# A two-layer mixture-of-experts block: how the gather's rows are copied out, where the seat tables are made, and the order around the router

## What is computed

```python
scores = softmax(x @ w_router + b_router)            # 16 experts in 4 groups of 4
g_sel = argmax(group_score)                          # group_score: sum of a group's two largest
top_w, top_i = top_k(scores within g_sel, 2)         # gate weights, renormalised
for e in range(16):
    h = silu(x @ w_gate[e]) * (x @ w_up[e])          # 1024 -> 512
    y = y + gate[:, e:e+1] * (h @ w_down[e])         # 512 -> 1024
```

## Time and profile before

| | us |
|---|---|
| median of 3 runs | 2279.32 |
| lowest, highest | 2276.93, 2283.09 |
| the profiled execution | 2278.92 |
| its span in the trace | 2277.1 |

### The profile page before, as it was taken

The page is one execution under the profiler, slowest core; times in us unless marked ns, Lnnn a source line. Parts: engine busy times, 40 slices in busy tenths (PEclk is TensorE's granted clock), DMA queues, the critical chain, the costliest instruction groups (busy, mean ns, idle before and its releaser), DMA issues.

```text
span 2277.1 us, 31229 instructions
## 1 busy us (share of the span) xinstructions
PE 2220.8 (98%) x13248; PEld 1916.0 (84%) x13248; DVE 1612.7 (71%) x1577; ACT 1286.8 (57%) x1360; POOL 57.9 (3%) x71
## 2 busy tenths in 40 slices
PE   8999999999999999999999999999999999799997
PEld 7888989788888889897888998887777998687775
DVE  6765855777477557466774666589999666689997
ACT  5434644554344446445543544578887555488885
POOL 1000100000000001000000000000000000100000
PEclk9999999999999999999999999999999999899999
DMA  7755443455555554434664555479998554399995
GB/s 243 218 186 169 148 139 126 163 186 187 193 174 185 188 180 134 152 129 164 199 191 168 181 185 185 141 283 384 385 382 330 181 185 167 131 338 383 388 374 198
DMA packets 309952, 490.93 MB, mean 216 GB/s; under 512 B 15504, under 2 KB 205120, under 8 KB 309808
## 3 DMA queue, kind: packets, MB, share of 16 engines
q1 hardware_dynamic: 305712, 475.35, 61.2%
q0 software_dynamic: 3104, 10.38, 1.6%
q10 hardware_dynamic: 992, 3.15, 0.4%
HBM read 487.40 MB, written 1.44 MB: 215 GB/s over the span
## 4 chain that ended last, share of the span: by engine, by line
PE 78%; DVE 10%; DMA 7%; ACT 3%; issue 2%; DVEq 0%; SPq 0%; ACTq 0%
PE PS L807 14%; PE PS L734 14%; PE PS L730 14%; PE PS L731 13%; PE PS L810 7%; DVE RL L2203 5%; DMA RINGS<-w_down 4%; DMA RINGS<-w_gate 3%; PE PS L1422 2%; ACT RH L1662 2%; PE PS L1419 2%; PE PS L1042 1%; PE PS L1007 1%; PE PS L981 1%; PE PS L992 1%
## 5 line engine op out<-in xcount | busy, mean ns | idle before, releaser
L2203 DVE TENSOR_TENSOR RL<-RINGS,RH 128x2048 fp32r<-128x2048 f32 x448 | 1011.3, 2272 | 421.5 <-ACT RH L1662 419.5
L1662 ACT ACTIVATE RH<-RINGS 128x2048 fp32r<-128x2048 f32 x447 | 848.6, 1900 | 453.2 <-PE PS L734 375.3
L807 PE MATMUL PS<-HTS,RH 128*128 128x512 f32 x1384 | 416.3, 397 | 1.2 <-DVE HTS L2189 1.2
L730 PE MATMUL PS<-RH,HTS 128*128 128x256 f32 (+1 forms) x1184 | 342.2, 305 | 0.4 <-DVE HTS L2185 0.4
L731 PE MATMUL PS<-RH,HTS 128*128 128x256 f32 (+1 forms) x1184 | 336.1, 300 | 0.0
L807 PEld LDWEIGHTS PS<-HTS,RH 128*128 128x128 f32 x1384 | 249.7, 189 | 48.7 <-issue 1.6
L810 PE MATMUL PS<-HTS,RL 128*128 128x256 f32 x1408 | 283.3, 281 | 0.0
L734 PE MATMUL PS<-RL,HTS 128*128 128x256 f32 (+1 forms) x1184 | 261.5, 299 | 0.0
L810 PEld LDWEIGHTS PS<-HTS,RL 128*128 128x128 f32 x1408 | 228.9, 188 | 15.2
L730 PEld LDWEIGHTS PS<-RH,HTS 128*128 128x128 f32 x1184 | 223.8, 189 | 11.9 <-issue 2.5
L731 PEld LDWEIGHTS PS<-RH,HTS 128*128 128x128 f32 x1184 | 224.7, 190 | 7.2
(11 more groups left out here) (463 smaller groups left out, 2969.3 us busy)
## 6 DMA issues: line engine op xcount, KB each, us to landing
...
```

The costliest lines, as they stand in the source:

```text
L730: mm(dst, a_[0], b_[0], start=start, stop=False)
L807: return mm(PS[:, bank + c, :], wh[:, k, c * P:(c + 1) * P], HTS[:, :, k, :], start=(k == 0), stop=(k == K - 1))
L1662: A(splits.buffer(RH, RH3)[:, 0:width], RINGS[:, slot, 0:width], ACT.Copy).then_inc(wh_ready, 1)
L2203: TTn(RL[:, slot, 0:width], RINGS[:, slot, 0:width], splits.buffer(RH, RH3)[:, 0:width].bitcast(F32), ALU.subtract).then_inc(wl_ready, 1)
```

## The change

The gather no longer sums rounded rows and rests. `gathered_rounded(k)` and `gathered_rests(k)` give the two kinds of product columns of their own, so that a bank holds one k block in the layout of XS, and a gather needs eight bank fillings of four banks: `gather(g, 0)` and `gather(g, 1)`, the second with a wait for the copy that frees the bank. ScalarE copies eight whole banks; VectorE's four subtractions are gone. `gather(0, 0)` stands before the branch, `gather(0, 1)` behind it. XL is made on VectorE (`rows_rest`) in place of GpSimd. The seat tables are made by group, in the first expert of each (bank 1 and 6 in place of 1, 3, 4, 5, 6), with their VectorE and ScalarE parts. The first weight splits of VectorE and ScalarE around the router move behind its chain, and in the second layer TensorE makes products that nobody reads (`idle_products`). The branch for crowded experts is adapted and not taken here.

```diff
-        def seat_parts(b, rest):
-
-            first = 64 if rest else 0
-            at = XS[:, 2 * b:2 * b + 2, 0, first:first + 1]
-            return bass.AP(tensor=at.tensor, offset=at.offset, ap=[*at.ap[:2], [2 * P, 2], [64 if rest else 192, 2], [1, 64]])
-
-        def seat_columns(b):
-
-            return PS[:, GBANK[b], :].rearrange("p (k q r n) -> p k q r n", k=2, q=2, r=2)
+        def gathered_rounded(k):
+
+            at = PS[:, GBANK[k % 4], 0:1]
+            return bass.AP(tensor=at.tensor, offset=at.offset, ap=[at.ap[0], [2 * P, 2], [192, 2], [1, 64]])
+
+        def gathered_rests(k):
+
+            return PS[:, GBANK[k % 4], :].rearrange("p (q n) -> p q n", q=2)[:, :, 64:192]
...
-                    if k == 2:
-                        for t in range(T):
-                            pool.wait_ge(xh_ready, T * l + t + 1)
-                            nc.gpsimd.tensor_tensor(XL[t], X[:, t, :], XH[:, t, :].bitcast(F32), ALU.subtract).then_inc(xl_ready, 1)
...
+                def idle_products(bank, count):
+
+                    for _ in range(count):
+                        mm(PS[:, bank, :], IDENT, CON[:, O_MB:O_MB + 512], start=True, stop=True)
+
                 splits.enter()
                 if l == 0:
                     unit_ahead(11, 2)
+                else:
+                    idle_products(3, 3)
...
                     unit_ahead(12, 5)
+                else:
+                    idle_products(5, 3)
...
+                else:
+                    idle_products(5, 1)
+
+                def gather(g, half):
+
+                    for k in range(4 * half, 4 * half + 4):
+                        if half:
+                            pe.wait_ge(seat_a, 8 * (l * NG_ + g) + k - 3)
+                        at = slice(k * P, (k + 1) * P)
+                        for t in range(T):
+                            mm(gathered_rounded(k), XH[:, t, at], SEATX[g][:, t, :].rearrange("p (q r n) -> p q r n", q=2, r=2), start=(t == 0), stop=(t == T - 1))
+                        for t in range(T):
+                            if g + k == 0:
+                                pe.wait_ge(xl_ready, T * l + t + 1)
+                            last = mm(gathered_rests(k), XL[t][:, at], SEATX[g][:, t, :].rearrange("p (q n) -> p q n", q=2), start=(t == 0), stop=(t == T - 1))
                         last.then_inc(gather_ready, 1)
...
-                pe.wait_ge(seat_ready, 2 * l + 1)
+                pe.wait_ge(seat_ready, 5 * l + 1)
                 pe.wait_ge(xh_ready, T * l + T)
-                gather(0)
+                gather(0, 0)
                 ring.experts = ring.n
...
-                    def seat_tables():
-
-                        pe.wait_ge(seat_ready, 2 * l + 2)
-                        if l == 0:
-                            pe.wait_ge(unit_a, taken_at(1, 12)[1])
-                        for i in range(NE // 2):
+                    def seat_tables(g):
+
+                        pe.wait_ge(seat_ready, 5 * l + 2 + g)
+                        for q in range(2):
                             for t in range(T):
-                                mm(PS[:, 4 + i // 4, i % 4 * P:(i % 4 + 1) * P], SEATX[i // 2][:, t, i % 2 * P:(i % 2 + 1) * P], SEATG[:, i // 2, t, :],
+                                mm(PS[:, 1, q * P:(q + 1) * P], SEATX[g][:, t, q * P:(q + 1) * P], SEATG[:, g, t, :], start=(t == 0), stop=(t == T - 1))
+                        for q in range(2):
+                            for t in range(T):
+                                mm(PS[:, 6, 2 * q:2 * q + 2], SEATX[g][:, t, q * P:(q + 1) * P].bitcast(F32), GATE[:, EG * g + 2 * q:EG * g + 2 * q + 2, t],
                                    start=(t == 0), stop=(t == T - 1))
-                        for i in range(NE // 2):
-                            for t in range(T):
-                                mm(PS[:, 6, 2 * i:2 * i + 2], SEATX[i // 2][:, t, i % 2 * P:(i % 2 + 1) * P].bitcast(F32), GATE[:, 2 * i:2 * i + 2, t],
-                                   start=(t == 0), stop=(t == T - 1))
-                        for j in range(NG_):
-                            for t in range(T):
-                                last = nc.tensor.transpose(PS[:, 1 + j // 2 * 2, ((j % 2) * T + t) * P:((j % 2) * T + t + 1) * P],
-                                                           SEATG[:, j, t, :].bitcast(F32), IDENT)
+                        for t in range(T):
+                            last = nc.tensor.transpose(PS[:, 1, (T + t) * P:(T + t + 1) * P], SEATG[:, g, t, :].bitcast(F32), IDENT)
                         last.then_inc(seat_tr, 1)
 
+                    gather(0, 1)
...
-                            pe.wait_ge(seat_d, 4 * (l * NG_ + g) + 2)
+                            pe.wait_ge(seat_a, 8 * (l * NG_ + g) + 4)
...
                         if j == 0:
-                            pe.wait_ge(seat_d, 4 * (l * NG_ + g) + 4)
+                            pe.wait_ge(seat_a, 8 * (l * NG_ + g) + 8)
                         stacked(0, 1, j)
-                        if e == 1:
-                            pe.wait_ge(seat_taken, l + 1)
+                        if j == 1:
+                            pe.wait_ge(seat_taken, l * NG_ + g + 1)
...
                         folded(0, e, CORG, 1)
-                        if e == 0:
-                            seat_tables()
-                        else:
+                        if j == 0:
+                            seat_tables(g)
+                        if e:
                             pe.wait_ge(eh_l, l * NE + e)
+                            if l == 0 and e == 1:
+                                pe.wait_ge(unit_a, taken_at(1, 12)[1])
                             if e > EG and j == 1:
                                 pe.wait_ge(y_l, l * 5 + g)
                             down_part(0, (e - 1) % EG == 0, False, 1)
                             if j == EG - 1 and g < NG_ - 1:
-                                gather(g + 1)
+                                pe.wait_ge(seat_ready, 5 * l + 3 + g)
+                                gather(g + 1, 0)
                             down_part(1, False, (e - 1) % EG == EG - 1, 1)
+                            if j == EG - 1 and g < NG_ - 1:
+                                gather(g + 1, 1)
...
-                split(back=3)
+                rows_rounded(1)
                 chunk()
                 A(RLT, PS[0:2 * NE, 4, 0:S], ACT.Copy).then_inc(rt_cols, 1)
                 A(EPS[:, 1:2], EPS[:, 0:1], ACT.Exp)
                 act.wait_ge(rt_in, l + 1)
                 A(SMALL[:, 256:288], SMALL[:, 256:288], ACT.Exp).then_inc(rt_exp, 1)
-                rows_rounded(1)
+                split(back=3)
...
-                    def gathered(g):
-
-                        for b in range(4):
-                            act.wait_ge(gather_ready, 4 * (l * NG_ + g) + b + 1)
-                            A(seat_parts(b, False), seat_columns(b), ACT.Copy).then_inc(seat_a, 1)
-
-                    def seats():
-                        act.wait_ge(seat_tr, l + 1)
-                        A(SEL.rearrange("p i n -> p (i n)"), PS[:, 4:6, :].rearrange("p b n -> p (b n)"), ACT.Copy)
-                        for i in range(2):
-                            last = A(SEATT[:, 2 * i:2 * i + 2].rearrange("p g t n -> p (g t n)"), PS[:, 1 + 2 * i, :], ACT.Copy)
-                        last.then_inc(seat_taken, 1)
+                    def gathered(g, half):
+
+                        for k in range(4 * half, 4 * half + 4):
+                            act.wait_ge(gather_ready, 8 * (l * NG_ + g) + k + 1)
+                            A(XS[:, k].rearrange("p j n -> p (j n)"), PS[:, GBANK[k % 4], :], ACT.Copy).then_inc(seat_a, 1)
+
+                    def seats(g):
+                        act.wait_ge(seat_tr, l * NG_ + g + 1)
+                        A(SEL[:, 2 * g:2 * g + 2, :].rearrange("p i n -> p (i n)"), PS[:, 1, 0:2 * P], ACT.Copy)
+                        A(SEATT[:, g].rearrange("p t n -> p (t n)"), PS[:, 1, 2 * P:4 * P], ACT.Copy).then_inc(seat_taken, 1)
...
+                        if j == 0:
+                            seats(g)
                         if e == 0:
-                            seats()
                             return
                         chunk()
                         split(back=3)
                         if j == EG - 1 and g < NG_ - 1:
-                            gathered(g + 1)
+                            gathered(g + 1, 0)
                         chunk()
+                        if j == EG - 1 and g < NG_ - 1:
+                            gathered(g + 1, 1)
...
+                    gathered(0, 0)
+                    gathered(0, 1)
...
-                    split()
-
+
+                def rows_rest(t):
+                    dve.wait_ge(xh_ready, T * l + t + 1)
+                    TTn(XL[t], X[:, t, :], XH[:, t, :].bitcast(F32), ALU.subtract).then_inc(xl_ready, 1)
+
+                rows_rest(0)
...
+                rows_rest(1)
...
-                gates()
```

(33 more changed lines are left out.)

33 lines of the change are left out of this document (10 added, 23 removed).

## The result

| | us, median | range | runs |
|---|---|---|---|
| before | 2278.39 | 2276.93 to 2283.09 | 4 |
| after | 2260.94 | 2259.02 to 2263.37 | 4 |

The ratio is 0.992, with a 95% interval of 0.9902 to 0.9939: the change makes the kernel 17.5 us faster. The forecast was 2263.5 us, in a range of 2257 to 2272.5; the direction, the range and most of the places were right, the size was 2.6 us short. The profiled execution of the changed kernel took 2259.02 us (span 2257.2), 19.9 us less than that of before; 15.3 were forecast.

What follows compares the result with a forecast made beforehand. Weight loads feed each expert phase, so only stretches where they stand still count. From 2278.92 us: -7.4 - 5.8 (layer 1) - 4.8 (layer 0) + 2.7 (groups) = -15.3, 2263.6, stated as 2263.5; range 2257 to 2272.5.

Steps and rivals of the forecast that it cites:

- Chain of the router: Layer 1's router: GpSimd's subtraction moved saves 2.1 us, earlier exponential 0.7, second subtraction 0.4; 3.6 us taken (2.0 to 4.5).
- Clock and idle products: Layer 1, before transposes, after scores and before places: seven unread products fill TensorE's pauses, costing nothing if the clock holds.
- The first rival: Layer 1's clock falls anyway: gather gives 0.8 instead of 3.8 us, idle products end 1.3 late; 2267.8 us, chance 0.13.
- First gather, layer 1: From first gather product to first expert's product: 4.0 us instead of 7.8, so 3.8 us go; branch taken as 0.
- the third rival: Scattered PSUM writes slow gather products; if doubled, 0.119 us more each, 30.5 us over eight groups: 2294 us, chance 0.06.
- Seat tables: First expert of each layer: 1.8 us of 7.55 stays; holes in the loads close, gaining 4.8 (layer 0) and 5.8 us.
- Layer 0: Start of its expert phase: the loads' hole closes, 4.8 us; 2.7 us of idle time before its first expert count nothing.
- Layer 1's start: Its experts start 7.4 us earlier (router 3.6, gather 3.8); closing a later stretch without loads gains 5.8 us more.
- the second hole: Layer 1, 2004 to 2010: loads stand nearly still (share 0.04), the full ring waiting for TensorE; closing it gains 5.8 us.
- Groups: Groups 1 to 3, both layers: each moved table costs 0.45 us, 2.7 in all; TensorE's 65.0 stays under the loads' 65.34.
- the second rival: Groups pay in full, since loads, ScalarE and VectorE follow one another: 1.8 us per table, 10.8 total; 2271.6 us, chance 0.14.
- The range: Kernel: chain 2.0 to 4.5 us, branch 0 to 1.1 twice, groups 0 to 10.8, holes 9 to 12: 2258 to 2271.

Runs made afterwards that it cites:

- tables_once: The changed kernel with the seat tables of all four groups back in the first expert: 2265.32 us, ratio 0.9960.
- both_undone: The changed kernel with old gather and old seat tables together, keeping the router chain and idle products: 2275.71 us, ratio 0.9991.

## Why the prediction was right, and where it was not

- **Chain of the router: right.** The choice ends 3.5 us earlier, counted from the layer's first load of w_gate (26.7 against 30.3 us; forecast 3.6): the stall of 2.1 us is gone, the exponential follows at once, the second subtraction lies beside the place products.
- **Clock and idle products: right.** Clock 1.00 throughout; without the products 0.54 and 4.3 us. The first rival's 4.3 us rest on a gather of 7.0 us at the low clock; by its own row (1.88 us for eight products) it would be 7.5 us.
- **First gather, layer 1: right.** 3.90 us, forecast 4.0. Branch and scattered writes cost nothing; the third rival, slower by scattered PSUM writes, falls: four runs of 64 float32 columns in PSUM cost no time in a product of 256 columns (0.12 us each, as before). The measurement differs here from the rule of the Trainium skill, "PSUM — Partial Sum Buffer", Specifications (TRN2), that any non-contiguous access pattern slows matmuls significantly, and it decides.
- **Seat tables: right in the first expert, 1.43 us instead of the 1.8 us of the sum.** The 10.7 us of tables_once against 10.6 are luck in part: 3.0 us in layer 0 for 4.8 and 7.7 (or 6.6) in layer 1 for 5.8.
- **Layer 0: the step that failed, 2.3 us.** Its start gains 7.1 us for a forecast of 4.8. The prediction took the length of the hole for the tables, and for the 2.7 us before the first expert: "loads run all through that stretch, so I count nothing for them". By stretches of 1 us the hole is 5.5 us long, since its edges lie outside the window of 5 us that was read: 0.7 us. And the loads ran, but slower: with a share of 1.01 they moved 358 GB/s where the changed kernel moves 394, which over 12 us is 1.1 us of loads. The kernel before, the changed kernel, and both_undone, which has a hole but no wait before its first expert:

```profile
1497.00:1509.00 12.00, 11.72 (x70) 10.18 (x70) 10.35 (x7) 9.51 (x9) 0.00 (x0) 1.00 1.01 358
1497.00:1509.00 12.00, 10.23 (x45) 7.65 (x44) 10.83 (x7) 10.63 (x10) 0.00 (x0) 0.92 1.04 394
1497.00:1509.00 12.00, 8.73 (x44) 7.16 (x42) 11.35 (x13) 7.84 (x8) 0.00 (x0) 0.86 1.04 394
```

  The remaining 0.5 us is open. That the wait is what slows the loads is the reading of one trace of each; no run puts this wait back alone.
- **Layer 1's start: right within the spread.** The first expert starts 8.05 us earlier (forecast 7.4) in both executions; the second hole gives 6.4 us in one and 5.3 us in the other, for 5.8.
- **Groups: the number right, the reason wrong.** 0.47 us per group (66.10 against 65.63 us on average) for 0.45. But TensorE's need does not stay beneath a fixed period of loads. TensorE waits 2.8 us per group for rests of weights (the changed kernel: 5.6 us in two groups), and yet 1.5 us more of products cost 1.5 us. That fits the mechanism of the second rival, that loads, ScalarE, VectorE and TensorE follow one another, at the present load already. So the 0.45 us, chosen between 0 and 1.8, was a lucky size.
- **The range.** Its upper end of 2271 us is not the sum of the bounds named for it: 1.6 us of chain, 2.2 of branch, 8.1 of groups and 1.6 of holes above 2263.5 are 2277. The measured time lies inside either.

The waits of the changed kernel in two groups, 1570 to 1702 (us in total, times, longest), which answer to the earlier trace rows:

```profile
DVE RL L2212 <- ACT RH L1669: 5.7, 6, 1.7
PEld PS L1425 <- DVE RL L2212: 5.6, 10, 1.0
ACT RH L1669 <- PE PS L728: 4.0, 5, 1.1
ACT RH L1669 <- DMA RINGS<-w_up: 3.9, 5, 0.9
```

ScalarE waits for TensorE (4.0 us) as long as for w_up (3.9 us): no one engine is the bound. Which order of waits closes this circle at 66 us, and why the first table costs 0.6 us and the second 1.5, stays open; the runs show the two slopes, not the link between them.
